# First attention: GpSimd's splits and products in pieces between its negations, and the low part of each finished pair moved to it

## The reference, cut to what matters

```python
def latent_attention(q, k_all, v_all):
    ...
    scale = HEAD_QK ** -0.5

    def one_block(qblk):
        s = jnp.einsum('bqhd,bkhd->bhqk', qblk, k_all, preferred_element_type=jnp.float32) * scale
        p = jax.nn.softmax(s, axis=-1).astype(v_all.dtype)
        return jnp.einsum('bhqk,bkhd->bqhd', p, v_all)
    ...

def merge_branches(f_mix, att, gates, w_fourier, w_mla_o, b_gate, w_out):
    g = jax.nn.sigmoid(gates + b_gate)
    g_f, g_a = g[..., :D_MODEL], g[..., D_MODEL:]
    y = g_f * (f_mix @ w_fourier) + g_a * (att @ w_mla_o)
    return y @ w_out
```

## Time and profile before

| | us |
|---|---|
| median of the runs | 3017.0 |
| the profiled execution's own time | 3021.57 |
| its span | 3019.8 |
| the attention loop within it, first to last negation and their neighbours | 455 to 727 |

### The profile page before, as it was taken

The page is one execution under the profiler, slowest core; times in us unless marked ns, Lnnn a source line. Parts: engine busy times, 40 slices in busy tenths (PEclk is TensorE's granted clock), DMA queues, the critical chain, the costliest instruction groups (busy, mean ns, idle before and its releaser), DMA issues. The chain is left out here.

```text
span 3019.8 us, 37184 instructions
## 1 busy us (share of the span) xinstructions
PE 2916.5 (97%) x14772; PEld 2424.8 (80%) x14772; DVE 1491.6 (49%) x2202; ACT 925.3 (31%) x1628; POOL 1108.4 (37%) x585
## 2 busy tenths in 40 slices
PE   7999999999999999999999999999899999999997
PEld 3877778888887888888888887788788888887786
DVE  5842237887644313122133444445626666664545
ACT  4122226675113101010011111420326555653411
POOL 1332351111586434444443443234343233322241
PEclk9999999999999999999999999999999999999998
DMA  5534574331533111111111111111142222221111
GB/s 239 188 129 142 191 235 137 86 89 48 190 122 112 50 49 49 49 50 49 50 49 49 49 63 56 42 42 49 54 165 63 73 66 71 69 71 50 37 49 63
DMA packets 123821, 263.00 MB, mean 87 GB/s; under 512 B 48476, under 2 KB 74540, under 8 KB 119424
## 3 DMA queue, kind: packets, MB, share of 16 engines
q1 hardware_dynamic: 123648, 260.57, 26.2%
HBM read 215.97 MB, written 46.06 MB: 87 GB/s over the span
## 5 line engine op out<-in xcount | busy, mean ns | idle before, releaser
L881 POOL TENSOR_TENSOR whi<-raw,onesf 128x1024 fp32r<-128x1024 f32 x187 | 362.0, 1936 | 1313.1 <-PE ps L439 1208.9
L437 PE MATMUL ps<-Hb_hi,whi 128*128 128x512 f32 x1424 | 572.6, 402 | 10.3 <-DVE Y L2846 5.9
L439 PE MATMUL ps<-Hb_hi,wlo 128*128 128x512 f32 x1424 | 556.0, 390 | 0.0
L438 PE MATMUL ps<-Hb_lo,whi 128*128 128x512 f32 x1424 | 554.9, 390 | 0.0
L883 POOL TENSOR_TENSOR wlo<-raw,whi 128x1024 fp32r<-128x1024 f32 x187 | 499.3, 2670 | 14.6
L437 PEld LDWEIGHTS ps<-Hb_hi,whi 128*128 128x128 f32 x1424 | 267.9, 188 | 62.6 <-issue 8.3
L439 PEld LDWEIGHTS ps<-Hb_hi,wlo 128*128 128x128 f32 x1424 | 267.2, 188 | 57.7
L438 PEld LDWEIGHTS ps<-Hb_lo,whi 128*128 128x128 f32 x1424 | 268.3, 188 | 48.0
L1907 ACT ACTIVATE tmp<-ps 64x256 f32<-64x256 f32 (+3 forms) x112 | 61.8, 552 | 535.9 <-PE ps L439 465.1
L1907 ACT ACTIVATE tmp<-tmp,mx 128x1280 f32<-128x1280 f32 (+2 forms) x192 | 187.1, 974 | 79.8 <-DVE mx L3121 50.3
L439 PE MATMUL ps<-Uhi,wlo 128*128 128x512 f32 x512 | 199.2, 389 | 0.0
(11 more groups left out here) (468 smaller groups left out, 5832.4 us busy)
## 6 DMA issues: line engine op xcount, KB each, us to landing
raw<-in_w SPq DMA_DIRECT2D x197, 512.0 KB, 3.5
adas<-in_ada SPq DMA_DIRECT2D x16, 1024.0 KB, 4.9
raw<-in_w SPq DMA_DIRECT2D x44, 256.0 KB, 3.7
adaE<-in_ada SPq DMA_DIRECT2D x4, 2048.0 KB, 23.2
gate_d<-gst SPq DMA_DIRECT2D x16, 512.0 KB, 2.8
v_d<-VS SPq DMA_DIRECT2D x2, 4096.0 KB, 14.2
ncB<-cum_d SPq DMA_DIRECT2D x16, 512.0 KB, 3.6
Vx<-v_d SPq DMA_DIRECT2D x16, 512.0 KB, 3.8
```

The lines of the kernel that those rows point to most:

```text
L437: nc.tensor.matmul(o, wh, xh, start=start, stop=False)
L438: nc.tensor.matmul(o, wh, xl, start=False, stop=False)
L439: return nc.tensor.matmul(o, wl, xh, start=False, stop=stop)
L881: nc.gpsimd.tensor_tensor(whi[b][:, 0:w], raw[b][:, 0:w], onesf[:, 0:1].to_broadcast([P, w]), ALU.mult).then_inc(S("split_hi"), 1)
```

## The change

Four things change, all in the attention's loop.

1. The two panels' splits are cut into halves of 128x512, one half ahead of each of neg(4) to neg(11): high of panel 0 in slots 4 and 5, low in 6 and 7, high of panel 1 in 8 and 9, low in 10 and 11.
2. A head's product is cut into four pieces of 64x256, ahead of neg(8h + 12) to neg(8h + 15). The first of them waits for `row_back`. Each is followed by a wait for its own end.
3. The low part of a finished pair moves from VectorE to GpSimd, in two halves of 128x512, ahead of neg(16i + 26) and neg(16i + 27) for pair i = 0, 1, 2.
4. The counts of `ml_inv` are renumbered for all engines, since a head now adds six to it and not three.

```diff
-MERGE_SPLITS = (4, 6, 8, 10)
+MERGE_AT = 4
...
-                    sp.wait_ge(S("ml_inv"), 3 * h + 2)
+                    sp.wait_ge(S("ml_inv"), 6 * h + 2)
...
+                def merge_half(n, low, c):
+                    if low:
+                        gp.wait_ge(S("split_hi"), n + 1)
+                        last = nc.gpsimd.tensor_tensor(wlo[n % 2][:, c], raw[n % 2][:, c], f32(whi[n % 2][:, c]), ALU.subtract)
+                    else:
+                        gp.wait_ge(S(f"loaded{n % 2}"), 16 * (n // 2 + 1 + twice(n)))
+                        gp.wait_ge(S("panel_done"), n - 1)
+                        last = nc.gpsimd.tensor_tensor(whi[n % 2][:, c], raw[n % 2][:, c], onesf[:, 0:1].to_broadcast([P, HALF]), ALU.mult)
+                    if c.stop == PW:
+                        last.then_inc(S("split" if low else "split_hi"), 1)
+
+                def product(h, p):
+                    r, c = slice(64 * (h % 2), 64 * (h % 2) + 64), slice(CTX * p, CTX * p + CTX)
+                    o = o32[h // 2 % 2][r, c]
+                    if p == 0:
                         gp.wait_ge(S("row_back"), 16 * (h + 1))
                         gp.wait_ge(S("ml_out"), 12 * h + 12)
+                    nc.gpsimd.tensor_tensor(o, o, rowsB[r, c], ALU.mult).then_inc(S("ml_inv"), 1)
+                    gp.wait_ge(S("ml_inv"), 6 * h + 3 + p)
+
+                def pair_lo(i, c):
+                    gp.wait_ge(S("ml_at"), 2 * i + 1)
+                    last = nc.gpsimd.tensor_tensor(At[1][:, i, c], o32[i % 2][:, c], f32(At[0][:, i, c]), ALU.subtract)
+                    if c.stop == T:
+                        last.then_inc(S("ml_at"), 1)
+
+                for t in range(SLOTS):
+                    if MERGE_AT <= t < MERGE_AT + 8:
+                        n, m = divmod(t - MERGE_AT, 4)
+                        merge_half(P0["merge"] + n, m // 2, slice(HALF * (m % 2), HALF * (m % 2) + HALF))
+                    if t >= 8 and t % 8 >= 4:
                         gp.wait_ge(S("ml_max"), t)
-                        nc.gpsimd.tensor_tensor(o, o, rowsB[64 * (h % 2):64 * (h % 2) + 64, :], ALU.mult).then_inc(S("ml_inv"), 1)
-                        gp.wait_ge(S("ml_inv"), 3 * h + 3)
+                        product(t // 8 - 1, t % 8 - 4)
+                    if t >= 16 and t % 16 in (10, 11):
+                        pair_lo(t // 16 - 1, slice(HALF * (t % 16 - 10), HALF * (t % 16 - 10) + HALF))
                     x = 8 * (t // 8 % 2) + t % 8
                     gp.wait_ge(S("ml_x"), 2 * t + 2)
                     nc.gpsimd.tensor_scalar(neg_max[:, x:x + 1], mx[:, 16 + t % 8:17 + t % 8], -1.0, None, ALU.mult).then_inc(S("ml_max"), 1)
...
-                    act.wait_ge(S("ml_inv"), 6 * i + 6)
+                    act.wait_ge(S("ml_inv"), 12 * i + 12)
                     copy(At[0][:, i, :], o32[i % 2][:, :], S("ml_at"))
...
-                def pair_lo(i):
-                    dve.wait_ge(S("ml_at"), 2 * i + 1)
-                    sub(At[1][:, i, :], o32[i % 2][:, :], At[0][:, i, :], S("ml_at"))
...
-                    if t >= 16 and t % 16 == 9:
-                        pair_lo(t // 16 - 1)
```

More of the change, by code:

```diff
@@ L1359, in flips @@
                         if g == 2 and t >= 8 and t % 8 == 0:
-                            pe.wait_ge(S("ml_inv"), 3 * (t // 8) - 2)
+                            pe.wait_ge(S("ml_inv"), 6 * (t // 8) - 5)
                             j = 8 * ((t // 8 - 1) % 2)
@@ L1377, in inverse_rows @@
                 def inverse_rows(h, t, b):
-                    pe.wait_ge(S("ml_inv"), 3 * h + 1)
+                    pe.wait_ge(S("ml_inv"), 6 * h + 1)
                     pe.wait_ge(S("ml_x"), 2 * t)
@@ L1427, in pe_program @@
                 attention_part(0, range(3))
-                pe.wait_ge(S("ml_inv"), 3 * NH + 1)
+                pe.wait_ge(S("ml_inv"), 6 * NH - 2)
                 fourier_part(0)
@@ L2108, in last_pair_hi @@
                     for n, c in enumerate(LAST_QUERIES):
-                        act.wait_ge(S("ml_inv"), 3 * NH + n)
+                        act.wait_ge(S("ml_inv"), 6 * NH - 3 + n)
                         copy(At[0][:, 3, c], o32[1][:, c], S("ml_at"))
@@ L2672, in inverse @@
                     if h:
-                        dve.wait_ge(S("ml_inv"), 3 * h)
+                        dve.wait_ge(S("ml_inv"), 6 * h)
                     nc.vector.reciprocal(inv_sum[:, x], row_sum[:, x]).then_inc(S("ml_inv"), 1)
-                def pair_lo(i):
-                    dve.wait_ge(S("ml_at"), 2 * i + 1)
-                    sub(At[1][:, i, :], o32[i % 2][:, :], At[0][:, i, :], S("ml_at"))
                 def last_product(n):
@@ L2683, in last_product @@
                     if n == 0:
-                        dve.wait_ge(S("ml_inv"), 3 * NH - 1)
+                        dve.wait_ge(S("ml_inv"), 6 * NH - 4)
                     dve.wait_ge(S("ml_out"), 12 * NH - 3 + 3 * n)
```

## The result

The changed kernel takes 3028.7 us (median of seven executions, 3027.2 to 3031.6), the kernel before 3017.0 (seven, 3014.7 to 3022.7): ratio 1.0036, 95% interval 1.0024 to 1.0047. Run again later beside other kernels it took 3029.2 against 3020.8: 1.0028, 1.0018 to 1.0037. It is 0.3% slower; the forecast was 3026.0 us, 0.30% slower.

The account below looks back on a forecast made before the run. Bound: in even slots, a chain without slack through GpSimd's negation, ScalarE and VectorE. Head 0 8.1 + five waits 6.6 - low parts 5.7 + clock 0 = +9.0 us, making the median 3026.0 us; range 3018 to 3035.

Parts of the forecast that it names:

- An even negation's delay is the kernel's, one for one: First attention's loop: even slots form a chain without slack, so delaying GpSimd's negation there delays the whole kernel equally.
- The five waits, 6.6 us: Heads 1 to 5: first quarter waits for rowsB ahead of neg(8h+12), 1.1 to 1.65 us each, 6.6 lost.
- The 4.27 from the issue to the negation: neg(8h+12) can't start before the rowsB transfer's issue + 3.44 + 0.74 + 0.09 us.
- Head 0, 8.1 us and 1.3 for the clock: neg(12) waits for late row sums: neg(14) at 522.68 against 514.53, 8.1 us lost; TensorE's clock fall adds 1.3.
- its 510: Sign of being wrong at head 0: neg(12) starting before 510 us in the changed profile.
- The low parts, 5.7 us: Pairs' low parts moved from VectorE to GpSimd: neg(26) sooner by 1.90 us, three times, 5.7 gained.
- The 0.37 that GpSimd's first half costs: Ahead of neg(26): first half piece waits for At_hi, moving the negation from 564.47 to 564.84.
- TensorE's clock, sum 0: TensorE in the loop: +1.3 us behind the neg(12) stall, -1.3 at slot 42; bounds -1.3 and +4.
- the -1.3 for slot 42: Slot 42 loses 2 of the 2.4 us its chain stood still, so 1.3 us of slow clock goes.
- The Trainium skill's rule against GpSimd: Low parts: two-input elementwise work belongs on VectorE, GpSimd about twice as slow; by the rule the move loses.
- The landings are sooner: Rival: row transfers land 2.4 us sooner, only head 0 waits; +2.4 us, 3019.4 us; chance 0.13.
- Faster: Rival: none of six heads waits for row sums, only gains remain; -10.4 us, 3006.6 us; chance 0.06.

Follow-up runs that it names:

- e1: Changed kernel with each head's product in two halves of 64x512 ahead of neg(8h+14) and neg(8h+15); 3016.2 us, ratio 0.9977 to the kernel before.
- e5: As e1, but head 0's two halves stand ahead of neg(16) and neg(17); 3008.9 us, ratio 0.9962 to the kernel before.
- e6: Changed kernel with SyncE's store of sums and load of rowsB ahead of head h+2's value load; 3024.6 us in one execution, before 3019.4.
- e7: As e6, but for head 0 the sums also go ahead of head 2's query and key loads; 3011.4 us, ratio 0.9970 to the kernel before.
- e2: Kernel before with only the pairs' low parts moved to GpSimd in two halves; 3012.1 us, ratio 0.9969 to the kernel before.
- e3: Kernel before with only the products cut in quarters ahead of neg(8h+12) to neg(8h+15); 3034.0 us, ratio 1.0038 to the kernel before.
- e8: As e7, with each pair's low part whole ahead of neg(16i+27); 3008.2 us, ratio 0.9957 to the kernel before.
- e10: As e5, with each pair's low part whole ahead of neg(16i+27); 3007.5 us, ratio 0.9955 to the kernel before.
- e4: Kernel before with only the two panels' splits in halves ahead of neg(4) to neg(11); 3023.0 us, ratio 0.9999 to the kernel before.

## Why the prediction was right, point by point

- *An even negation's delay is the kernel's, one for one.* Right. Each wait shows undiminished in the stretch that holds it, and e1, e5, e6 and e7 take it away there.
- *The five waits, 6.6 us.* Right: 1.33 + 1.22 + 1.41 + 1.48 for heads 1, 2, 3, 5, and 1.07 for head 4 if the slow stretch of before there is taken as 1.39; the sum is 6.5. The 4.27 from the issue to the negation was 4.25 at head 1.
- *Head 0, 8.1 us and 1.3 for the clock.* The mechanism was right, the size too large: neg(14) came 65.97 us behind neg(0), before 59.27, so 6.7 and not 9.4 (8.3 in the second profile). The train did move as one piece (first quarter 17.12 us behind the panel load, the product before 17.48), and neg(12) to neg(14) took 9.84, the 8.36 and 1.5 for the clock. What was mis-sized is where the train starts. I had neg(10) come 0.9 us sooner; it came 3.5 sooner (36.71 behind neg(0), before 40.21). Of the 2.6 us between, 1.0 is an earlier landing of the first panel, and 1.6 is the slow stretch of TensorE behind neg(4), which the profiled execution of before had and which no other execution here has: neg(4) to neg(10) takes 24.82 to 24.87 in all eleven others, those of e2 and e3 with whole splits among them. I built on a stretch that belonged to one execution. So one of the prediction's signs of being wrong did show: neg(12) starts at 509.30, ahead of its 510 (forecast 514.32). Of the 5.0 us, 2.1 come from an earlier neg(0) (453.17, before 455.26), 2.6 from neg(10) as above, and the rest from the slightly shorter train. The sign was set on an absolute time, which moves with all that stands ahead of the loop; the wait that it was to test is there, with GpSimd idle for 13.55 us.
- *The low parts, 5.7 us.* Right: 1.92 + 1.62 + 1.87 = 5.4. The 0.37 that GpSimd's first half costs was about right too, by e8 and e10 (0.3 to 0.35).
- *TensorE's clock, sum 0.* The fall behind slot 12 came, and cost 1.5 us in one profile and 2.8 in the other, where 1.3 was forecast. The fall behind a stall of 2 us is less regular than two sightings suggested, so the -1.3 for slot 42 was no dependable gain. The low part on VectorE stops TensorE for the same 2 us at slots 42 and 58; in the kernel before the slow stretch came behind the first of them, in e4 behind the second. At slot 58 the same 20 matmuls with the values took TensorE 2.63 us in the kernel before and 3.69 in e4:

```profile
704.33 2.63 PE L1374 MATMUL ps<-Ea,Va 128*128 128x256 f32 x20 [1.97 <-DVE mx L2652]
```

```profile
703.01 3.69 PE L1379 MATMUL ps<-Ea,Va 128*128 128x256 f32 x20 [1.99 <-DVE mx L2657]
```

- *The Trainium skill's rule against GpSimd (GPSIMD Engine Reference, section 4.1).* The ratio of about two held (1.23 us on VectorE, 2 x 1.30 on GpSimd), the conclusion didn't: e2 alone is 0.3% faster than before.
- *The landings are sooner.* This rival didn't come: the store takes 3.60 to 3.92 us at heads 1 to 5 of the changed kernel, and all five quarters wait. Rows show for the same 4 KB store 1.2 us with nothing just ahead of it, 3.5 to 4.3 behind a 640 KB load, and 7.1 to 9.9 at head 0 behind head 2's loads. The Trainium skill's fixed 2.0 us (DMA: Bandwidth & Descriptors, Anatomy of one DMA) is stated for DMAs that GpSimd issues; these are SyncE's, and the figure lies between their times. So what decided was what stood ahead in the queue.
- *Faster.* This rival did not come about, but with the waits gone (e5, e7, e8, e10) the medians lie 9 to 13 us below the kernel before, where it had -10.4.

The sum for the loop was +9.0; the two profiles of the changed kernel gave +6.6 and +8.6, the medians +11.7 and +8.4. The mechanism was right at every place. That the total came out so near is in part luck: head 0's term was 2.6 us too large at its start, in the second profile the clock gave 1.5 of that back, and the rest of the kernel moves by 5 us between executions.

## What to carry to other kernels

Cutting a long instruction into pieces lets it start earlier, but if its place in the order moves ahead with it, so does its wait, and everything queued behind then waits for data that the old place had given time to land. Before moving work on an in-order engine, put the landing time of its last input beside the start of the instruction that will stand behind it; here five of seven places were late by a little over a microsecond and one by eleven. And order small transfers that something waits for ahead of large ones that nothing waits for yet: moving the store and load of the sums forward in SyncE's list turned the same GpSimd order from 0.3% slower into 0.3% faster.

## What the runs showed of the hardware

- A 4 KB store to DRAM comes back in 1.21 to 1.51 us with no load issued just ahead of it (head 6 in every profile, heads 1 to 5 in e6, e7 and e8), in 3.5 to 4.3 us behind a 640 KB load, in 2.7 to 2.8 behind two panel loads (e7 and e8, head 0), and in 7.1 to 9.9 us behind head 2's loads as well (the longest in e10).
- GpSimd's pieces cost 0.72 to 0.75 us for 64x256, 1.26 to 1.30 for 64x512, 1.30 for 128x512 with two full inputs, 1.04 for a 128x512 rounding copy (1.90 for 128x1024). Cut in four, the 2.39 us product takes 4 x 0.735 = 2.94.
- The landing of the first panel moves by some 2 us from one execution to another (neg(0) to neg(4) between 11.5 and 13.8 us over twelve executions), and the unchanged rest of the kernel by 5. Differences of less than that between two single profiles are no evidence; stretches of a few slots are, which repeat to 0.1 us where TensorE's clock stays up.
- Behind the stalls of 9 to 11 us ahead of neg(12) TensorE's granted clock was a mix of 2.4 and 1.2 GHz each time: from neg(12) to neg(14) a mean of 0.70 and 0.60 in the changed kernel's two profiles, 0.65 in e3 and 0.67 in e6. Behind shorter ones it fell in some executions only, and the length didn't decide: with TensorE idle for 1.67 us it fell in e2 (0.83 from neg(14) to neg(16)), with 2.40 at the same place in the kernel before it stayed at 1.00.
